# Weight chunks split inside the FFN that ends a layer, chunk 2 split ahead of the gate copies, and layers unrolled, in a two-network transformer kernel

## What is computed

```
def reference(x, ...):
    for i in range(2):                                     # network A
        x = x + hybrid_mixer(rmsnorm(x, norm1_g[i]), w_in[i], ...) @ w_out[i]
        a, u = split(rmsnorm(x, norm2_g[i]) @ w_up[i])     # 2 x 2816 columns
        x = x + (silu(causal_conv3(a)) * u) @ w_down[i]
    x = rmsnorm(x, final_g)
    for l in range(2):                                     # network B
        mod = silu(c) @ ada_w[l] + ada_b[l]                # 3 sub-blocks x (shift, scale, gate)
        for sub, f in enumerate((ffn 0, token_mixer, ffn 1)):
            y = f(x * (1 + scale) + shift)
            x = layer_norm(2 ** 0.5 * x + (0.5 or 1) * (1 + gate) * y, ln_g[l, sub], ln_b[l, sub])
    return x
```

## Time and profile before

| what | value |
|---|---|
| median of 3 runs | 2173.15 us (2167.86 to 2176.16) |
| profiled execution | 2177.1 us, span 2175.4 us |
| TensorE busy (matmul) | 1975.5 us, 91% of the span |
| VectorE busy | 1381.4 us, 64% |
| ScalarE busy | 963.8 us, 44% |
| GpSimd busy | 147.4 us, 7% |
| mean granted TensorE clock | 0.943 of full |
| moved by DMA | 373.22 MB, 172 GB/s mean |

### The profile page before, as it was taken

The page is one execution under the profiler, slowest core; times in us unless marked ns, Lnnn a source line. Parts: engine busy times, 40 slices in busy tenths (PEclk is TensorE's granted clock), DMA queues, the critical chain, the costliest instruction groups (busy, mean ns, idle before and its releaser), DMA issues.

```text
span 2175.4 us, 36223 instructions
## 1 busy us (share of the span) xinstructions
PE 1975.5 (91%) x13906; PEld 1847.0 (85%) x13906; DVE 1381.4 (64%) x2155; ACT 963.8 (44%) x1479; POOL 147.4 (7%) x202
## 2 busy tenths in 40 slices
PE   7988999798899969998998989995999898898997
PEld 7878999797899959997887979995999788887996
DVE  4486788538677867667646565446776764746455
ACT  4455444445544444444544343433434545334432
POOL 0000000000000000002003320000000200512000
PEclk9998999889999989999998899997999999989999
DMA  7116676411577657863420145546776241024552
GB/s 270 44 57 253 248 301 250 142 62 59 189 286 286 255 214 285 302 230 120 147 92 1 59 138 192 192 156 237 268 279 226 101 167 57 1 97 154 178 190 78
DMA packets 54109, 373.22 MB, mean 172 GB/s; under 512 B 5984, under 2 KB 6880, under 8 KB 10848
## 3 DMA queue, kind: packets, MB, share of 16 engines
q1 hardware_dynamic: 51392, 361.45, 46.1%
q0 software_dynamic: 2016, 9.07, 1.2%
q10 hardware_dynamic: 576, 0.99, 0.1%
HBM read 370.45 MB, written 1.05 MB: 171 GB/s over the span
## 4 chain that ended last, share of the span: by engine, by line
PE 80%; DVE 12%; ACT 5%; issue 2%; DMA 1%; DVEq 0%; ACTq 0%; POOLq 0%; SPq 0%
PE bank L610 17%; PE bank L611 17%; PE bank L612 17%; PE bank L673 5%; PE bank L674 5%; PE bank L675 5%; DVE w_lo L1487 2%; PE bank L1030 2%; PE bank L1039 1%; PE bank L1038 1%; PE bank L626 1%; DVE scratch L1481 1%; ACT w_hi L1101 1%; DVE scratch L2042 1%; DVE scratch L1889 1%
## 5 line engine op out<-in xcount | busy, mean ns | idle before, releaser
L610 PE MATMUL bank<-hT_hi,w_hi 128*128 128x256 f32 x2432 | 702.6, 289 | 33.9 <-DVE scratch L1521 23.9
L1487 DVE TENSOR_TENSOR w_lo<-raw,w_hi 128x2048 fp32r<-128x2048 f32 (+2 forms) x270 | 618.4, 2292 | 139.5 <-ACT w_hi L1101 139.1
L611 PE MATMUL bank<-hT_lo,w_hi 128*128 128x256 f32 x2432 | 696.9, 287 | 0.0
L612 PE MATMUL bank<-hT_hi,w_lo 128*128 128x256 f32 x2432 | 696.3, 286 | 0.0
L1101 ACT ACTIVATE w_hi<-raw 128x2048 fp32r<-128x2048 f32 (+2 forms) x270 | 508.9, 1886 | 197.0 <-PE bank L675 120.1
L610 PEld LDWEIGHTS bank<-hT_hi,w_hi 128*128 128x128 f32 x2432 | 473.9, 195 | 41.8 <-DVE w_lo L1487 36.4
L611 PEld LDWEIGHTS bank<-hT_lo,w_hi 128*128 128x128 f32 x2432 | 473.7, 195 | 4.3 <-issue 1.4
L612 PEld LDWEIGHTS bank<-hT_hi,w_lo 128*128 128x128 f32 x2432 | 473.5, 195 | 0.5
L610 PE MATMUL bank<-w_hi,hT_hi 128*128 128x256 f32 (+2 forms) x800 | 234.7, 293 | 2.0 <-DVE hT_lo L1504 2.0
L611 PE MATMUL bank<-w_lo,hT_hi 128*128 128x256 f32 (+2 forms) x800 | 232.7, 291 | 0.0
L612 PE MATMUL bank<-w_hi,hT_lo 128*128 128x256 f32 (+2 forms) x800 | 232.4, 291 | 0.0
(11 more groups left out here) (352 smaller groups left out, 2361.9 us busy)
## 6 DMA issues: line engine op xcount, KB each, us to landing
raw<-in_wb SPq DMA_DIRECT2D x168, 1024.0 KB, 5.0
raw<-in_wa SPq DMA_DIRECT2D x96, 1024.0 KB, 4.8
scratch<-in_wm SPq DMA_DIRECT2D x72, 1024.0 KB, 6.5
lnw<-in_ln_g POOLq DMA_DIRECT2D x6, 512.0 KB, 3.9
lnw<-in_ln_b POOLq DMA_DIRECT2D x6, 512.0 KB, 5.9
cst<-in_const POOLq DMA_DIRECT2D x1, 2205.0 KB, 9.4
raw<-in_wa SPq DMA_DIRECT2D x4, 512.0 KB, 3.5
scratch<-in_c SPq DMA_DIRECT2D x4, 512.0 KB, 4.4
```

Source lines behind the costliest of these rows:

```text
L610: nc.tensor.matmul(out, ah, bh, start=(i == 0), stop=False)
L611: nc.tensor.matmul(out, ah, bl, start=False, stop=False)
L612: last = nc.tensor.matmul(out, al, bh, start=False, stop=(i == n - 1))
L1487: nc.vector.tensor_tensor(w_lo[:, slot, 0:width], raw[:, raw_slot, 0:width], w_hi[:, slot, 0:width].bitcast(F32), ALU.subtract).then_inc(l ...
```

## The change

1. *Layers unrolled.* Each `Fori(0, DEPTH)` becomes a Python loop, so that each layer has its own code and constants in the place of registers. Every engine but GpSimd and SyncE gets a `drain` behind its wait for `layer_go`. `spa` holds the small parameters of both A layers and is loaded once, ahead of A0; `layer["first"]` picks the columns.
2. *First chunks split in the FFN that ends a layer.* `more` becomes 2 (ScalarE) and 1 (VectorE) for the A FFNs and for FFN 1 of B0. The splits at a layer's start (`hi_a(0)`, `hi_a(1)`, `lo_a(0)`, `hi_b(0)`, `hi_b(1)`, `lo_b(0)`) go, but for the first layer of all. In B `lo_mod` comes ahead of `gate_diagonal`.
3. *Chunk 2 earlier.* ScalarE's gate copies and silu of c move into the FFN as `start`, behind the high part of chunk 2. VectorE makes chunk 2's low part ahead of the six `ada` products and not in tile 0's `post`.
4. The eight PSUM banks are one tensor instead of eight.

```
-            with pe.Fori(0, DEPTH) as l:            # the same on all engines, both networks
+            for l in range(DEPTH):
+                layer["first"] = l
...
                 pe.wait_ge(layer_go, l + 1)
+                pe.drain()                          # also scalar and vector, both networks
...
-        spa = sb("spa", [P, max(SA_W, SB_W)])
+        spa = sb("spa", [P, max(DEPTH * SA_W, SB_W)])
...
+            a += layer["first"] * SA_W
...
                 hi(split + 2, 2, 2, raw0 + 16)      # scalar, ffn
+                start()
                 post(0, 0, 0, 0, lambda: hi(split + 3, 0, 0, raw0 + 32))
...
-                act.dma_start(spa[:, 0:SA_W], t["sa"][bass.ds(l, 1), :, :].rearrange("o p n -> (o p) n")).then_inc(small_in, 16)
-                hi_a(0)
-                act.wait_ge(small_in, l * 16 + 16)
+                if l == 0:
+                    act.dma_start(spa[:, 0:DEPTH * SA_W].rearrange("p (l n) -> p l n", l=DEPTH),
+                                  t["sa"].rearrange("l p n -> p l n")).then_inc(small_in, 16)
+                    hi_a(0)
+                    act.wait_ge(small_in, 16)
                 hi_features(A, 0, "g1")
-                hi_a(1)
+                if l == 0:
+                    hi_a(1)
...
-                silu_c(l + 1)
-                ffn(A, split + (A_WIN + A_WOUT), l * (16 * A_N // RING) + 16 * (A_N0["ffn"] // RING), 0, True, 0)
+                ffn(A, split + (A_WIN + A_WOUT), l * (16 * A_N // RING) + 16 * (A_N0["ffn"] // RING), 0, True, 2,
+                    lambda: silu_c(l + 1))
...
-                hi_b(0)
                 hi_mod(0, 0)
-                hi_b(1)
-                gate_copy(0)
-                silu_c(l + (DEPTH + 1))
-                ffn(B, split, l * (16 * B_N // RING) + 16 * N_A, 0, False, 2)
+
+                def gate_and_c():
+                    gate_copy(0)
+                    silu_c(l + (DEPTH + 1))
+
+                ffn(B, split, l * (16 * B_N // RING) + 16 * N_A, 0, False, 2, gate_and_c)
...
-                gate_copy(2)
-                ffn(B, split + B_S0["ffn1"], l * (16 * B_N // RING) + 16 * (N_A + B_S0["ffn1"] // RING), FT, False, 0)
+                ffn(B, split + B_S0["ffn1"], l * (16 * B_N // RING) + 16 * (N_A + B_S0["ffn1"] // RING), FT, False,
+                    2 if l + 1 < DEPTH else 0, lambda: gate_copy(2))
...
                 lo(split + 1, 1, 1)                 # vector, ffn
+                lo(split + 2, 2, 2)
                 if part is not None:
                     dve.wait_ge(c_silu, part + 1)
                     for k in range(2 * RING):
                         ada(0, k)
-                post(0, 0, 0, lambda: lo(split + 2, 2, 2))
+                post(0, 0, 0, lambda: None)
...
-                lo_a(0)
-                dve.wait_ge(small_in, l * 16 + 16)
+                if l == 0:
+                    lo_a(0)
+                    dve.wait_ge(small_in, 16)
...
-                ffn(A, split + (A_WIN + A_WOUT), 0, 0, conv=True, part=l)
+                ffn(A, split + (A_WIN + A_WOUT), 0, 1, conv=True, part=l)
...
+                lo_mod(0, 0)
                 gate_diagonal(0)
-                lo_b(0)
-                lo_mod(0, 0)
                 ffn(B, split, 0, 2, part=l + DEPTH)
...
-                ffn(B, split + B_S0["ffn1"], FT, 0)
+                ffn(B, split + B_S0["ffn1"], FT, 1 if l + 1 < DEPTH else 0)
```

More of the change, by code:

```diff
@@ L350, in build @@
         ident = const("ident")
+        layer = {"first": 0}
         def sa(name, i=None):
             a, w = SA[name]
+            a += layer["first"] * SA_W
             return spa[:, a:a + w] if i is None else spa[:, a + i:a + i + 1]
         def conv_tap(f, i):
-            return spa[:, bass.ds(f * 4 + (SA["conv"][0] + i), 1)]
+            return spa[:, bass.ds(f * 4 + (layer["first"] * SA_W + SA["conv"][0] + i), 1)]
         def sbp(name, i=None):
@@ L490, in _ @@
             sp.dma_start(cst[:, 0:P], t["const"][:, 0:P]).then_inc(x_in, 16)
-            with sp.Fori(0, DEPTH) as l:
+            for l in range(DEPTH):
                 for n in range(A_N0["ffn"]):
@@ L547, in _ @@
             pool.dma_start(lnw[:, 0, :], t["final_g"].partition_broadcast(P)).then_inc(start_in, 16)
-            with pool.Fori(0, DEPTH) as l:
+            for l in range(DEPTH):
                 for v in (rw, kbd, vr, pc):
@@ L695, in ffn @@
                 down(FT - 2, 0, FFN_N - 1, (FFN_N - 1) % RING, last_one=True)
-            with pe.Fori(0, DEPTH) as l:
+            for l in range(DEPTH):
+                layer["first"] = l
                 split = l * A_S
@@ L837, in _ @@
                 pe.wait_ge(layer_go, l + 1)
+                pe.drain()
             pe.wait_ge(start_in, 32)
             pe.wait_ge(FIN["x"], TT)
-            with pe.Fori(0, DEPTH) as l:
+            for l in range(DEPTH):
                 split = l * B_N + S_A
@@ L1115, in hi_features, with ffn @@
                                          scale=sa(gain, k) if gain else 1.0).then_inc(N["tp_hi"], 1)
-            def ffn(N, split, raw0, h0, conv, more):
+            def ffn(N, split, raw0, h0, conv, more, start=lambda: None):
                 def hi_at(pos, slot):
@@ L1164, in _ @@
             root_mean_square(NEXT, 0)
-            with act.Fori(0, DEPTH) as l:
+            for l in range(DEPTH):
+                layer["first"] = l
                 split = l * A_S
@@ L1277, in _ @@
                 act.wait_ge(layer_go, l + 1)
+                act.drain()
             def hi_mod(v, sub):
@@ L1555, in ffn @@
                 post(FT - 1, 1, 1, (lambda: lo(split + FFN_N, 0, 0)) if more else (lambda: None))
-            with dve.Fori(0, DEPTH) as l:
+            for l in range(DEPTH):
+                layer["first"] = l
                 split = l * A_S
@@ L1827, in _ @@
                 dve.wait_ge(layer_go, l + 1)
+                dve.drain()
             normed(NEXT, DEPTH, FIN, 0)
```

7 lines of the change are left out of this document (4 added, 3 removed).

## The result

The changed kernel took 2156.89 us (median of 4 runs, 2156.36 to 2157.31) beside 2174.65 us for the kernel before on the same chip; the ratio is 0.9927, with a 95% interval of 0.9907 to 0.9947. The forecast was 2156.0 us in a range of 2147 to 2167. The profiled execution of the changed kernel has a span of 2155.4 us, against 2175.4.

A forecast was written before the change was run, and what follows sets the result against it. TensorE's own work was taken as four fifths of the chain that ended last, so only its stalls or lower clock pay. Won 30.0 us, paid 12.9, net 17.1: profiled 2177.1 to 2160.0, median 2156, range 2147 to 2167.

The forecast's parts named there:

- The jumps: Hand-overs A0 to A1 and B0 to B1: unrolling removes the jump to the loop's head, winning 3.13 and 3.9 us.
- A0 to A1 behind the reciprocal: Reciprocal to first product at A0 to A1: chunk 0's splits and `spa`'s load no longer stand between, 1.38 us won.
- FFN 0 in B: Start of FFN 0, both B layers: 3.96 us from splits and gate diagonal, 2.24 from chunk 2's low part; 6.2 each.
- FFN 1 in B: Start of FFN 1, both B layers: TensorE's 2.9 us wait and 1.7 us of lower clock go, 9.2 us together.
- Rival 1: FFN 1 in B: GpSimd gets between the two low parts, the 9.2 us stay away, 2165 us; chance 0.12.
- Ends of the A FFNs: Last feature tile's `post` holds both splits: 1.64 us later plus a clock drop of 1.7; cost 2 x 3.3 us.
- The end of B0's FFN 1: It gets the splits FFN 0 already has, so TensorE waits 1.7 us instead of 0.5; cost 1.2 us.
- Starts of the A FFNs: Chunk 2's low part ahead of `ada`, 2.24 us, against `h32` 1.64 us sooner behind the tap: 0.6 us late, twice.
- The first load: Run's start: `spa` now holds both layers, 182 KB more, costing up to 6.3 us; 3.5 us taken.
- Drains: One after each of three inner layer ends, 0.1 us each; cost 0.3 us.
- Rival 4: Tails and first load cheap: no clock drop (3.4 us back), load free (3.5 back), 2149 us; chance 0.09 including still faster.

The follow-up runs named there:

- Run 2: Unrolling alone against the kernel before: layers unrolled, drains, one load of `spa`; splits and chunk 2 where they stood; 2167.58 us, ratio to before 0.9971.
- Run 3: Changed kernel without splits at the FFN ends: each layer splits chunks 0 and 1 itself, gate diagonal first; 2157.13 us, ratio to before 0.9924.
- run 4: Changed kernel with chunk 2 late again: split behind the gate copies, its low part behind the first modulations; 2166.56 us, ratio to before 0.9972.
- Run 6: Changed kernel with the splits at FFN ends behind `hid_hi` and `hid_lo` instead of ahead of `h32`, all layers; 2152.03 us, ratio to before 0.9907.
- run 5: Changed kernel with `spa` loaded layer by layer instead of both layers at once; 2159.71 us, ratio to before 0.9939.
- run 10: Changed kernel with the end splits behind `hid_hi` and `hid_lo` only in both A layers and FFN 1 of B0; 2150.97 us, ratio to before 0.9893.
- run 9: The changed kernel a third time, unmodified, as yardstick; 2155.28 us, ratio to before 0.9911.
- run 1: The changed kernel again, unmodified, as yardstick; 2151.59 us, ratio to before 0.9897.
- Run 11: On top of run 10: first feature tile ahead of all six modulation products in B, behind two in A; 2136.13 us, ratio to before 0.9815.

## Why the prediction came out right

**The jumps** (3.13 + 3.9 us): right. Run 2, with hardly anything but them (the drains and the one load of `spa` are in it too), measured 3.2 and 3.5 in their segments. What in the jump takes the time no run shows; unrolling also puts constants in the place of registers.

**A0 to A1 behind the reciprocal** (1.38 us): in the timeline 6.44 - 5.62 = 0.8 us were won. VectorE's scaling of `x` takes 1.97 us there, at the time of GpSimd's clears, which may be what is missing; that was not tried apart.

**FFN 0 in B** (2 x 6.2 us): 6.5 in B0 (5.6 against run 2), and 6.5 in B1 (210.65 against 217.13 in run 2). The working has one slip: it compared the gate path with that of FFN 1, 9.41 us, but FFN 0 took 10.12; its transposes alone are 3.65 us there and 3.37 in FFN 1. This slip and the 0.8 us that unrolling won in B0's segment (run 2) cancel, which is luck. The wait for `h32`, 4.7 us, was forecast as 4.8. Run 3 puts 3.7 and 4.5 us on the splits (forecast 3.96), run 4 3.0 and 2.1 on chunk 2 (forecast 2.24).

**FFN 1 in B** (2 x 4.6 us): right, also in the mechanism, low parts first and GpSimd behind them. Run 4 gives 4.65 and 4.69. Rival 1, GpSimd between the low parts, has fallen. The Trainium skill (SBUF — State Buffer, SBUF: two separate sides) has a GpSimd instruction and a VectorE one with two SBUF inputs exclude each other for a whole instruction; the trace agrees, for the exclusion only moved, to `hid_lo` with its 4.17 us, and there TensorE did not wait for it.

**Ends of the A FFNs** (2 x 3.3 us, of them 1.7 of clock): about right in size. Run 6 takes it apart into 1.6 and 1.6 us at A0; it gains 3.4 and 3.2 over run 5, run 10 2.7 and 3.2 over run 9. Run 3, with no splits at all, gains only 1.7 at A0 and 2.8 at A1, since at A0 the lower clock stayed behind a wait of 2.12 us. So the clock's share is not owed to the longer wait alone; what decides it is open. The end of B0's FFN 1 (1.2 us) shows as 1.2 in run 3.

**Starts of the A FFNs** (2 x 0.6 us): too small in A0, where run 4 gives 2.1, about right in A1 with 0.3. `h32` is late by 0.6 us at both, as worked out (19.1 us behind A0's norm, 18.5 before and in run 4). The rest at A0 is clock: in the 10 us from 15 us behind its norm it is 1.00 in run 4 and 0.83 in run 1, 1.7 us, while at A1 it is 0.83 in both. Unrolling also won 1.4 us in the segment of A1's FFN, clock as well (run 2), and 0.8 in B0's FFN 0, which no term had.

**The first load** (3.5 us): wrong. The working took 9.7 - 5.49 us, the difference between two loads at different places of the run, as the price of their bytes; but the same 303 KB that took 9.7 us before took 7.1 in the changed kernel. Twice the bytes at the same place took 0.4 us more (run 5). It is the mis-sized term: without it the sum is 20.6 us, of which 19.6 fall in the FFN segments, and these show 21.0.

**Drains** (0.3 us): below what the segments can tell.

Rival 4, ends and first load cheap, was right in its second half; it had 0.09. The median fell on the forecast within 1 us partly by chance: the terms give 20.6 with the load put right, and the three series gave 17.8, 21.5 and 17.7 us. The prediction counted what the change pays at the A ends, and the wait that the `ada` products leave ahead of `h32`, but did not ask whether either has to be paid. Run 11 turns them into 19 us more.

## What to carry to other kernels

Put work for the next stage behind the last instruction that somebody waits for, unless the next stage needs it at once: at the A ends that won 2.7 to 3.4 us each, at FFN 0 of B it lost 0.9 and 1.0. A TensorE stall of 2 to 4 us can cost its wait and some 1.7 us more, for the lower clock behind it; a stall of 2.1 us at the end of A0's FFN had that price in two runs and not in a third, so look at the clock of each. Before an instruction is put off, look for the DMA queue that waits for it and for what stands behind that wait: here products put off held a weight chunk back by 10 us, and a reorder meant to win 15 us lost 33. To judge a part of a change, mark segments at instructions that every version has: five of six repeated within 0.1 us where the medians of one kernel, on three chips, lay 5 us apart.

## What the runs showed of the hardware

- Unrolling, which removes the jump back to the head of a long loop body, won 3.2 us (A0 to A1, VectorE late) and 3.5 us (B0 to B1, TensorE late) of their segments; from root to reciprocal, with drains and clears between, straight-line code that runs for the first time took 0.77 us, with the jump 3.99.
- A load of 364 KB issued 8.1 us into the run took 6.1 us, one of 182 KB at the same place 5.7.
- Two VectorE low parts queued back to back (4.49 us) ran ahead of a GpSimd instruction issued 0.23 us behind the first; that and a second one took 13.53 us together, against 11.24 with one low part ahead. A VectorE instruction that takes 0.42 us elsewhere took 4.17 while GpSimd was still at work.
- Behind a TensorE wait of 2.12 us at the same instruction, products took 0.63 us each for some 3 us in two runs (3 and 10) and 0.39 in a third (6).
- One stretch of 50 us in a mixer, with nearly the same waits (9.1 and 9.5 us), had a granted clock of 0.86 in the kernel before and 0.97 in the changed one. By its segment the mixer took 268.2 us before and 264.7 to 264.9 in four executions of the changed kernel (one of them run 5's); it took 264.0 to 268.2 in the other versions: a few us that a change elsewhere moves, in both directions.
